# A block of x turned two steps behind its convolution, and column copies and the last row scaling placed ahead of the attention's steps

## The chip, the cores and the metric

One core of a Trainium2 chip runs the kernel. The metric is device microseconds of the whole program, the median of three runs: 4026.04 us (4020.71 to 4030.5). The engines are TensorE (PE, which multiplies and transposes into PSUM), VectorE (DVE), ScalarE (ACT), GpSimd (POOL) and SyncE (SP, which here only issues loads of weights). All data is 32-bit float.

## The reference, cut to what matters

The model is one large mixer layer with mixture-of-experts, followed by two smaller layers. The change lies in the mixer of the large layer. From the normed input h (512 tokens, 1024 wide, with 256 context tokens beside it) a projection makes, among others, x, B, C and z of a state-space branch (SSD) and q, k, v of a neighbourhood attention (NA).

```
xbc = silu(dwconv(xbc, conv_w, conv_b))       # 5-tap convolution along the tokens
xs, Bm, Cm = split(xbc)                       # xs: 2048 channels = 4 groups of 512
states, y   = chunked scan of xs, dt, A, Bm, Cm   # chunks of 128 tokens, both directions
u = y * silu(z);  u = u * rsqrt(mean(u*u) + eps)  # per group of 512: the row scaling
o_na = neighbourhood_attention(rope(q), rope(k), v, ...)   # 16 heads, 8 x 64 grid
```

The convolution runs along tokens, so x is made with channels on the partitions. The scan wants tokens on the partitions, so each block of 128 channels is transposed ("turned") afterwards.

## The kernel before, in words

Each engine has a program written out by hand, a chain of Python generators. `pace` advances a main generator (the scan's steps, later the attention's steps) and puts so many steps of a filler generator ahead of each main step, by a list (PLAN0, PLAN1). Every engine runs its own share of the same steps in the same order; semaphores tie them together. An engine executes its instructions in the order of its program, so whatever stands behind a waiting instruction waits too.

**SSD projections.** `pe_proj`, `act_proj` and `dve_proj` treat one group of 512 channels in eight steps: four steps of x (one per block of 128 channels) and four of z. A block i of x goes through: `pe_conv` on PE (16 products with the weights, 2 PSUM banks), `act_pad` on ACT (two copies to SBUF, L742 and L745), `dve_conv` on DVE (five instructions, L768 and L772), `act_silu` on ACT (L753, L756), `pe_turn_x` on PE (six transposes, 2 banks, L319), and then `dve_turn_x` (L987) and `act_turn_x` (L953), which copy the turned block out and free its two banks. After the blocks PE turns B (two banks, copied out by DVE at L1002), and multiplies z in four tiles (L307, one bank each).

**The scan** of the group before is the main work meanwhile: `pe_chunks`, `act_chunks`, `dve_chunks`, `pool_chunks`, fifteen steps per group. Five state steps are followed by ten steps n = 0 to 9. PLAN0 puts one filler step ahead of each of the first three state steps and ahead of n = 0, 2, 4, 6 and 8. The four x steps of the next group stand at n = 0, 2, 4, 6; its first z step stands at n = 8, and z tiles 1 to 3 at the state steps of its own scan. In step n DVE runs `dve_second(n-2)`, `dve_first(n)` and `dve_join(n-2)`. `dve_join` (L1303) waits for three additions of POOL (L1334, L1337, L1340), which wait for POOL's product M (L1324), which waits for ACT's exponential (L1149), which waits for a select of DVE (L1275) that stands behind the convolution of the same step. ACT squares the joined row (L1180) and then comes to the next silu. PE's `pe_second` (L1090) needs M, and its L1097 products feed `dve_second`. The first state product (L1061) needs x weighed by DVE (L1050), which needs all four turned blocks.

**PSUM.** There are eight banks. `open_bank` takes the least recently used one of a pool's banks and waits until its last user has been copied out. For group 0 the x steps use all eight banks; after the fifth step the list is set to the four banks 0 to 3 (PG1), while the scan uses 4 to 7. So from then on a tile takes the bank of the tile four places before it. The last tiles of a group in the order before are: x3 (2 banks), turned block 2 (2), B (2), z0, z1, turned block 3 (2), z2, z3. Group 0's `dt` work (`pe_dt`, `act_dt`, `dve_dt`) stands between its fifth and sixth step.

**Into the attention.** After the last scan step every engine runs what is left of the filler (the rope of q and k, number 1, rows 2 and 3), then the NA attention's steps. The V products (`pe_na_v`, at L307) need HTn, a copy of the input with its columns in another order: ACT makes the odd tiles (`act_by_blocks`, L1776) and DVE the even ones (`dve_by_blocks`, L1782), as the first thing of their V filler, in attention step 1. `dve_scale_z` (L1208 to L1218) scales the rows of the last SSD group in step 3, and PE then turns them (`pe_finish_last`, L319), with ACT copying each out (L1189). POOL fills the near tables (`pool_near_zero`, `pool_near_edge` L1738, `pool_near_mid` L1748) and then takes its last two rope products (L1583).

Of the kernel before, what the change touches and what calls it, by code (L numbers as in the profile page):

```python
# [189 lines left out]
def build(nc, A, out):  # L190
    ctx = ExitStack()
    with ctx:
# [738 lines left out]

        def pe_proj(pe, g, pool):
            for i in range(4):
                pe_conv(pe, ("x", g), i, pool)
                if i:
                    pe_turn_x(pe, g, i - 1, pool)
                yield
            pe.wait_ge(*at("conv", "BF", g))
            for part, n in ((0, 4), (4, 2)):
                pe_turn(pe, ("tb", g, part), pool, [BF[:, g, (part + c) * 128:(part + c + 1) * 128] for c in range(n)], "pe_turn")  # L940
            for n, _ in enumerate(pe_gemm(pe, ("z", g), 8, 512, range(4), lambda i, kt, w: HT[:, kt, i * 128:(i + 1) * 128],
                                          lambda i, kt, w: w, pool, "pe_z")):
                if n == 1:
                    pe_turn_x(pe, g, 3, pool)
                yield

# [9 lines left out]
        def act_proj(act, g):  # L956

            def silu(i):
                prev = ("tx", g, i - 2, 4) if i > 1 else ("tx", g - 1, i + 2, 4)
                before = [("full", prev)] if g or i > 1 else []  # L960
                if g == 0 and i == 1:
                    before = [("full", ("BF", 3, 2))]
                act_silu(act, ("x", g), i, 4 * g + i, xsF[i % 2][:, 0:512], xsF[i % 2][:, 512:768], before)

            for i in range(4):
                if i:
                    silu(i - 1)
                act_pad(act, ("x", g), i)
                if i:
                    act_turn_x(act, g, i - 1)  # L970
                yield
            silu(3)
            zs = zs2[g % 2]
            for i in range(4):
                act.wait_ge(*at("full", (("z", g), i)))
                if i == 0 and g > 1:
                    act.wait_ge(*at("full", ("fin", g - 2, 3)))
                act.activation(zs[:, i, :], PS.of((("z", g), i)), ACT.Silu, bias=0.0, scale=1.0).then_inc(
                    *up(S("act_z"), ("free", (("z", g), i)), ("zs", g, i)))
                if i == 1:  # L980
                    act_turn_x(act, g, 3)
                yield

# [5 lines left out]

        def dve_proj(dve, g):  # L990
            for i in range(4):
                if i == 1 and g > 1:
                    dve.wait_ge(*at("gone", g - 2, "pool"))
                    dve.wait_ge(*at("gone", g - 2, "pe"))
                if i:
                    dve_turn_x(dve, g, i - 1)
                dve_conv(dve, ("x", g), i, 4 * g + i)
                yield
            for part, n in ((0, 4), (4, 2)):
                key = ("tb", g, part)  # L1000
                dve.wait_ge(*at("full", key))
                dve.tensor_copy(BT2[g % 2][:, part:part + n, :], r3(PS.of(key)[:, 0:n * 128], 128)).then_inc(  # L1002
                    *up(S("dve_xs"), ("free", key), ("bt", g, part)))
            for i in range(4):
                if i == 1:
                    dve_turn_x(dve, g, 3)
                yield
# [342 lines left out]
        def act_finish_last(act):  # L1350
# [1 line left out]
            for part in range(2):  # L1352
                act_finish(act, 3, part)
            yield

        def dve_finish_last(dve):
            dve_scale_z(dve, 3)
            yield from idle(2)

# [460 lines left out]

        def act_na_v(act, m):
            if m == 0:
                act_by_blocks(act)
                act.wait_ge(*at("gone", 3, "pool"))
            for i in range(6):
                if i % 2:
                    key = (("v", m), i)
                    act.wait_ge(*at("full", key))  # L1830
                    act.activation(nv2[m][:, i, :], PS.of(key), ACT.Copy, bias=0.0, scale=1.0).then_inc(*up(S("act_v"), ("free", key), ("V", m, i)))
                yield
# [21 lines left out]
        def dve_na_v(dve, m):  # L1854
            if m == 0:
                dve_na_rope(dve, 1, 3)
                dve_by_blocks(dve)
                dve.wait_ge(*at("gone", 3, "pool"))
            for i in range(6):
                if i % 2 == 0:  # L1860
                    key = (("v", m), i)
                    dve.wait_ge(*at("full", key))
                    dve.tensor_copy(nv2[m][:, i, :], PS.of(key)).then_inc(*up(S("dve_v"), ("free", key), ("V", m, i)))
                yield
# [1182 lines left out]
        def act_program(act):  # L3047
            act_start(act)
            act_ssd_rows(act)
            weave(act_bc(act), act_ada_rest(act), 1)  # L3050
            proj = act_proj(act, 0)
            weave(take(proj, 5), act_dt(act), 0.5)
            filler = chain(proj, *[act_proj(act, g) for g in (1, 2, 3)], act_na_qk(act, 0), act_na_qk(act, 1))
            pace(chain(*[act_chunks(act, g) for g in range(4)]), filler, PLAN0, False)
            wait_all(act, CHUNKS_END)
            act.wait_ge(*at("rpb"))
            act.dma_start(ncon, nsrc).then_inc(*up(S("near_in"), by=16))
            act_near_raw(act, 0)
            V0 = act_na_v(act, 0)
            pace(act_att_2(act, NEAR), chain(filler, take(V0, 2), act_finish_last(act), V0, act_na_v(act, 1), act_na_qk(act, 2), act_na_qk(act, 3), act_branch_ssd(act)), PLAN1)  # L3060
            run(act_gates(act, "n", 1))
            act_out1(act)
            act_router(act)
            act_gather(act, 0)
            act_tables(act)
            for m in range(8):
                act_experts(act, m)
            act_moe_end(act)
            for L in range(2):
                if L == 0:  # L3070
                    act_first_of_0(act)
                else:
                    act_between(act)
                pace(act_att_2(act, CAUSAL[L]), chain(*[act_proj_2(act, L, n) for n in (1, 2, 3)]), PLAN2)
                act_last_out_2(act, L)
                if L:
                    act.wait_ge(*at("attn_end", L))
                    act.dma_start(gf, A["g_final"].partition_broadcast(128)).then_inc(*up(S("gf_in"), ("gf",), by=16))
                act_mlp(act, L)
            act_end(act)  # L3080

        def dve_program(dve):
            last_conv[0] = None
            dve_start(dve)
            dve_ssd_pads(dve)
            weave(dve_bc(dve), dve_ada_rest(dve), 1)
            proj = dve_proj(dve, 0)
            weave(take(proj, 5), dve_dt(dve), 0.5)
            filler = chain(proj, *[dve_proj(dve, g) for g in (1, 2, 3)], dve_na_qk(dve, 0), dve_na_qk(dve, 1, 0))
            pace(chain(*[dve_chunks(dve, g) for g in range(4)]), filler, PLAN0, False)  # L3090
            wait_all(dve, CHUNKS_END)
            V0 = dve_na_v(dve, 0)
            pace(dve_att_2(dve, NEAR), chain(filler, take(V0, 2), dve_finish_last(dve), V0, dve_na_v(dve, 1), dve_na_qk(dve, 2), dve_na_qk(dve, 3, 2), dve_branch_ssd(dve)), PLAN1)
            dve_branch_na(dve)
            dve_out1(dve)
            dve_router(dve)
            dve_places(dve, 0)
            dve_gather(dve, 0)
            for m in range(8):
                dve_experts(dve, m)  # L3100
            dve_moe_end(dve)
            for L in range(2):
                if L == 0:
                    dve_first_of_0(dve)
                else:
                    dve_between(dve)
                pace(dve_att_2(dve, CAUSAL[L]), chain(*[dve_proj_2(dve, L, n) for n in (1, 2, 3)], dve_out_2(dve, L)), PLAN2)
                dve_last_out_2(dve, L)
                dve_mlp(dve, L)
            dve_end(dve)  # L3110

        def pool_program(pool):
            pool_start(pool)
            filler = chain(idle(27), pool_na_qk(pool, 0), pool_na_qk(pool, 1))
            pace(chain(*[pool_chunks(pool, g) for g in range(4)]), filler, PLAN0, False)
            pool_near_zero(pool)
            pool_near_edge(pool, 0)
            pool_near_mid(pool, 0)
            pace(pool_att_2(pool, NEAR), chain(filler, idle(14), pool_na_qk(pool, 2), pool_na_qk(pool, 3), idle(20)), PLAN1)
            pool_branch_na(pool)  # L3120
            pool_out1(pool)
            pool_places(pool, 0)
# [51 lines left out]
```

## Time and profile before

| | |
|---|---|
| median of 3 runs | 4026.04 us |
| profiled execution | 4025.7 us, its span 4023.9 us |
| PE busy | 3660.3 us (91%) |
| DVE / ACT / POOL busy | 1148.0 / 772.9 / 441.4 us |
| mean granted clock of PE | 0.969 |

Times in the rows are microseconds from the span's start. A timeline row holds start, duration, engine, line, operation, tiles and count, and in brackets the idle time of that engine before it and what ended it. A product of one 128x128 block by 512 columns is recorded as two matmuls, so a tile of eight products shows x16. The granted clock is 1.00 at 2.4 GHz and 0.50 at 1.2 GHz. The change touches the stretch from about 215 to 810 us.

### The profile page before, as it was taken

The numbers are of one execution on the slowest core, as the hardware profiler recorded it, in microseconds if no ns is written. First come the engines' busy times: TensorE is split into PE (matmuls) and PEld (weight loads), VectorE is DVE, ScalarE is ACT, GpSimd is POOL, SyncE is SP. The second block draws the span as 40 slices with busy tenths as digits, with TensorE's granted clock in tenths as the row PEclk, the third lists the DMA queues.
The fourth block names the chain that finished last, engine by engine and source line by source line (L and its number), as shares of the span: only waits on it lengthen the run. The fifth ranks groups of instructions, "written<-read, shape, count | busy, mean of one in ns | idle before, by whom it ended". The sixth has DMA issues, their size and how long they took to land.

```text
span 4023.9 us, 32988 instructions
## 1 busy us (share of the span) xinstructions
PE 3660.3 (91%) x12600; PEld 1766.6 (44%) x12600; DVE 1148.0 (29%) x2602; ACT 772.9 (19%) x1778; POOL 441.4 (11%) x397
## 2 busy tenths in 40 slices
PE   6888899899999887888888888899999999999999
PEld 3355454444444433333233334555444445554444
DVE  2345555424210220311101114543221134432211
ACT  2024444322210200000000002332110123221100
POOL 1002223302100000000000001101221011012210
PEclk8899999999999999999999998999999999999999
DMA  8322223211222479999999991102222120022220
GB/s 253 126 72 79 69 84 94 69 58 37 79 71 96 174 283 409 409 409 409 409 409 409 409 392 54 37 27 84 84 77 75 57 84 32 32 96 67 84 71 34
DMA packets 302154, 634.08 MB, mean 158 GB/s; under 512 B 32499, under 2 KB 145763, under 8 KB 301743
## 3 DMA queue, kind: packets, MB, share of 16 engines
q1 hardware_dynamic: 240480, 591.96, 39.3%
q10 hardware_dynamic: 61519, 40.02, 3.6%
q8 instruction: 102, 1.67, 0.2%
q14 instruction: 53, 0.43, 0.0%
HBM read 625.50 MB, written 10.24 MB: 158 GB/s over the span
## 4 chain that ended last, share of the span: by engine, by line
PE 52%; DMA 19%; DVE 3%; ACT 1%; issue 1%; POOL 0%; SPq 0%; DVEq 0%; ACTq 0%
PE psum L307 26%; DMA arena<-in_w_exp_up_dram 7%; DMA arena<-in_w_exp_gate_dram 7%; PE psum L1572 6%; DMA arena<-in_w_exp_down_dram 4%; PE psum L2851 4%; PE psum L2815 4%; PE psum L2357 3%; PE psum L1396 2%; PE psum L2836 1%; PE psum L1424 1%; PE psum L2306 1%; PE psum L1405 1%; PE psum L2275 1%; PE psum L2750 1%
## 5 line engine op out<-in xcount | busy, mean ns | idle before, releaser
L307 PE MATMUL psum<-arena 128*128 128x512 f32 (+1 forms) x3200 | 1302.6, 565 | 7.6 <-DVE arena L1782 5.0
L307 PEld LDWEIGHTS psum<-arena 128*128 128x128 f32 x3200 | 609.8, 192 | 682.2 <-issue 653.6
L2357 PE MATMUL psum<-arena 128*64 128x512 f32 x3072 | 693.7, 596 | 153.0 <-DMA arena<-in_w_exp_up_dram 76.5
L2357 PEld LDWEIGHTS psum<-arena 128*64 128x64 f32 x3072 | 233.3, 136 | 594.6 <-issue 574.1
L1572 PE MATMUL psum<-arena 128*128 128x512 f32 x768 | 351.9, 613 | 0.0
L732 PE MATMUL psum<-arena 128*128 128x512 f32 (+1 forms) x768 | 269.8, 511 | 1.3 <-ACT arena L550 1.3
L1572 PEld LDWEIGHTS psum<-arena 128*128 128x128 f32 x768 | 147.5, 196 | 193.8 <-issue 192.9
L1504 DVE CUSTOM_DVE_ANT_0 arena<-psum,arena 128x512 f32<-128x512 f32 (+3 forms) x224 | 113.9, 546 | 387.0 <-PE psum L1396 386.8
L2894 POOL TENSOR_SCALAR arena<-arena 128x512 f32<-128x512 f32 x88 | 138.4, 1572 | 696.5 <-ACT arena L2873 696.5
L732 PEld LDWEIGHTS psum<-arena 128*128 128x128 f32 x768 | 151.0, 199 | 125.1 <-issue 114.5
L2900 DVE SCALAR_TENSOR_TENSOR arena<-arena 128x512 f32<-128x512 f32 x88 | 66.2, 753 | 426.5 <-POOL arena L2894 426.5
L1444 ACT ACTIVATE arena<-arena 128x512 f32<-128x512 f32 (+3 forms) x224 | 134.3, 601 | 138.5 <-DVE arena L1504 137.9
L2422 DVE TENSOR_TENSOR arena<-arena,psum 128x512 f32<-128x512 f32 x32 | 22.0, 689 | 461.7 <-PE psum L2357 461.7
L2851 PE MATMUL psum<-arena 128*128 128x512 f32 x352 | 152.0, 592 | 0.0
L2815 PE MATMUL psum<-arena 128*128 128x512 f32 x352 | 151.7, 592 | 0.0
L2873 ACT ACTIVATE arena<-psum 128x512 f32<-128x512 f32 x88 | 52.5, 597 | 509.8 <-PE psum L307 478.3
L1405 PE MATMUL psum<-arena 128*128 128x128 f32 x576 | 86.1, 278 | 56.0 <-DVE arena L1511 30.7
L1583 POOL TENSOR_TENSOR arena<-arena 128x512 f32<-128x512 f32 x48 | 62.3, 1300 | 588.0 <-ACT arena L1579 588.0
L319 PE MATMUL psum<-arena 128*128 128x128 f32 (+2 forms) x442 | 68.0, 303 | 61.6 <-ACT arena L756 27.4
L1405 PEld LDWEIGHTS psum<-arena 128*128 128x128 f32 x576 | 68.8, 143 | 107.1 <-DVE arena L1511 38.1
L2815 PEld LDWEIGHTS psum<-arena 128*128 128x128 f32 x352 | 66.6, 189 | 84.7 <-issue 84.7
L1396 PE MATMUL psum<-arena 64*128 64x512 f32 (+6 forms) x448 | 103.4, 543 | 0.0
(283 smaller groups left out, 2946.7 us busy)
## 6 DMA issues: line engine op xcount, KB each, us to landing
arena<-in_w_exp_gate_dram SPq DMA_DIRECT2D x128, 1024.0 KB, 18.8
arena<-in_w_exp_up_dram SPq DMA_DIRECT2D x128, 1024.0 KB, 18.5
arena<-in_w_exp_down_dram SPq DMA_DIRECT2D x128, 1024.0 KB, 18.8
arena<-in_w_in_dram SPq DMA_DIRECT2D x64, 1024.0 KB, 5.3
arena<-in_w_up_dram SPq DMA_DIRECT2D x88, 512.0 KB, 4.8
arena<-in_w_ada_dram SPq DMA_DIRECT2D x24, 1024.0 KB, 8.5
arena<-in_w_down_dram SPq DMA_DIRECT2D x20, 1024.0 KB, 5.1
arena<-acs_scratch ACTq DMA_DIRECT2D x64, 256.0 KB, 3.7
```

What stands on the lines that cost most here:

```text
L307: mm = pe.matmul(shaped(b, l, r), l, r, start=kt == 0, stop=kt == nkt - 1)
L319: t = pe.transpose(b[0:m, c * k:(c + 1) * k], x, ident[0:k, 0:k])
L732: mm = pe.matmul(b[:, 0:z - a], wt(nm, kt, 512)[:, i * 128:(i + 1) * 128], HT[:, kt, a:z], start=kt == 0, stop=kt == 7)
L1396: pe.matmul(b[:, 0:u.nk], J.queries(u, a, z), J.keys(u, a, z), start=True, stop=True).then_inc(*up(S("pe_score"), ("full", ("s2", J.id, i, ...
L1405: t = pe.transpose(b[:, 128 * j:128 * j + 128], J.score(i, c)[:, 128 * j:128 * j + 128], ident)
L1444: act.activation(J.score(i, c), J.score(i, c), ACT.Exp, bias=sv2(i, c)[:, 0:1], scale=-1.0, accum_out=sv2(i, c)[:, 1:2]).then_inc(*up(S("a ...
L1504: dve.tensor_tensor_reduce(out=J.score(i, c), in0=PS.of(("s2", J.id, i, c))[:, 0:u.nk], in1=J.table(u, c), scale=-J.scale(u), scalar=3.0e3 ...
L1572: mm = pe.matmul(b, wt(nm, kt, 256)[:, i * 128:(i + 1) * 128], src[:, kt, 0:512], start=kt == 0, stop=kt == 7)
L2357: mm = pe.matmul(banks[n][64 * j:64 * j + 64, :], lhs[:, kt, 64 * j:64 * j + 64], w, start=kt == 0, stop=kt == 2 * nkb - 1)
L2815: mm = pe.matmul(banks[i], actT[:, kt, i * 128:(i + 1) * 128], wt(nm, kt, 512), start=kt == 0, stop=kt == 21)
L2851: mm = pe.matmul(b, actT[:, kt, i * 128:(i + 1) * 128], wt(nm, kt, 512), start=kt == 0, stop=kt == 21)
L2894: pool.tensor_scalar(accs3[n % 4], pads3[n % 4][:, 0:512], w3(L, 0, ti_of(s, i)), None, ALU.mult).then_inc(*up(S("pool_acc"), ("acc3", L, n)))
```

## The change

In `pe_proj`, `act_proj` and `dve_proj` block i-2 is turned at step i, before block i's own convolution (on PE) or pad copies (on ACT) or convolution (on DVE), instead of block i-1 after or before it. Block 2 is turned at the start of the fifth step. PE and ACT turn block 3 with z tile 0, in the fifth step; DVE copies its share of block 3 in the sixth step, as before. The column copies move from the V filler to ahead of the attention, behind the near tables' loads on ACT; on DVE the row scaling of the last group moves there too, behind the copies. POOL takes one rope product ahead of the near tables and one behind them, before the attention's first step.

```diff
         def pe_proj(pe, g, pool):
             for i in range(4):
+                if i > 1:
+                    pe_turn_x(pe, g, i - 2, pool)
                 pe_conv(pe, ("x", g), i, pool)
-                if i:
-                    pe_turn_x(pe, g, i - 1, pool)
                 yield
+            pe_turn_x(pe, g, 2, pool)
             pe.wait_ge(*at("conv", "BF", g))
...
-                if n == 1:
+                if n == 0:
                     pe_turn_x(pe, g, 3, pool)
...
             for i in range(4):
                 if i:
                     silu(i - 1)
+                if i > 1:
+                    act_turn_x(act, g, i - 2)
                 act_pad(act, ("x", g), i)
-                if i:
-                    act_turn_x(act, g, i - 1)
                 yield
             silu(3)
+            act_turn_x(act, g, 2)
...
-                if i == 1:
+                if i == 0:
                     act_turn_x(act, g, 3)
...
         def dve_proj(dve, g):
             for i in range(4):
-                if i == 1 and g > 1:
+                if i == 2 and g > 1:
                     dve.wait_ge(*at("gone", g - 2, "pool"))
                     dve.wait_ge(*at("gone", g - 2, "pe"))
-                if i:
-                    dve_turn_x(dve, g, i - 1)
+                if i > 1:
+                    dve_turn_x(dve, g, i - 2)
                 dve_conv(dve, ("x", g), i, 4 * g + i)
                 yield
+            dve_turn_x(dve, g, 2)
...
-        def dve_finish_last(dve):
-            dve_scale_z(dve, 3)
-            yield from idle(2)
...
         def act_na_v(act, m):
             if m == 0:
-                act_by_blocks(act)
...
         def dve_na_v(dve, m):
             if m == 0:
                 dve_na_rope(dve, 1, 3)
-                dve_by_blocks(dve)
...
             act_near_raw(act, 0)
+            act_by_blocks(act)
...
+            dve_by_blocks(dve)
+            dve_scale_z(dve, 3)
             V0 = dve_na_v(dve, 0)
-            pace(dve_att_2(dve, NEAR), chain(filler, take(V0, 2), dve_finish_last(dve), V0, ...
+            pace(dve_att_2(dve, NEAR), chain(filler, take(V0, 2), idle(2), V0, ...
...
             pool_near_zero(pool)
+            run(take(filler, 1))
             pool_near_edge(pool, 0)
             pool_near_mid(pool, 0)
-            pace(pool_att_2(pool, NEAR), chain(filler, idle(14), ...), PLAN1)
+            run(take(filler, 1))
+            pace(pool_att_2(pool, NEAR), chain(filler, idle(14), ...), [0] + PLAN1[1:])
```

## Rows read from the trace of the kernel before

**Rows 1.** The page's first part: busy time, share and instructions.
```profile
PE 3660.3 (91%) x12600; PEld 1766.6 (44%) x12600; DVE 1148.0 (29%) x2602; ACT 772.9 (19%) x1778; POOL 441.4 (11%) x397
```

**Rows 2.** The waits of PE, 240 to 840 us: total, times, longest.
```profile
PE psum L319 <- ACT arena L756: 27.4, 9, 4.9
...
PE psum L1061 <- DVE arena L1050: 5.5, 4, 1.4
PE psum L319 <- DVE arena L1218: 5.3, 1, 5.3
PE psum L307 <- DVE arena L1782: 5.0, 1, 5.0
```

**Rows 3.** Timeline, 340 to 350 us: from silu 0 of group 1 to the next convolution.
```profile
345.99 0.49 ACT L756 ACTIVATE arena<-arena 128x256 f32<-128x256 f32 x1
...
346.87 0.37 ACT L745 ACTIVATE arena<-psum 128x256 f32<-128x256 f32 x1
...
347.69 0.69 DVE L987 COPY arena<-psum 128x512 f32<-128x512 f32 x1 [9.35 <-PE psum L319]
...
348.30 0.61 DVE L768 TENSOR_SCALAR arena<-arena 128x772 f32<-128x772 f32 x1
```

**Rows 4.** Timeline of DVE: what follows the join at n = 7, groups 1, 2, 3.
```profile
403.32 1.01 DVE L1002 COPY arena<-psum 128x512 f32<-128x512 f32 x2
...
525.17 1.01 DVE L1002 COPY arena<-psum 128x512 f32<-128x512 f32 x2
...
646.59 1.01 DVE L1002 COPY arena<-psum 128x512 f32<-128x512 f32 x2
```

**Rows 5.** Timeline of PE: B turned, z0, second 6 and 7 with L1097, z1 of group 2.
```profile
517.37 0.82 PE L319 MATMUL psum<-arena 128*128 128x128 f32 x6
518.03 7.04 PE L307 MATMUL psum<-arena 128*128 128x512 f32 x16
524.91 1.89 PE L1090 MATMUL psum<-arena 128*128 128x64 f32 x16
...
528.41 7.04 PE L307 MATMUL psum<-arena 128*128 128x512 f32 x16
```

**Rows 6.** Timeline of PE: z0 of group 1, and the first state products of groups 1, 2, 3.
```profile
392.90 7.05 PE L307 MATMUL psum<-arena 128*128 128x512 f32 x16
...
416.40 1.99 PE L1061 MATMUL psum<-arena 128*128 128x512 f32 x4 [1.39 <-DVE arena L1050]
...
537.49 1.99 PE L1061 MATMUL psum<-arena 128*128 128x512 f32 x4 [1.38 <-DVE arena L1050]
...
659.73 1.99 PE L1061 MATMUL psum<-arena 128*128 128x512 f32 x4 [1.39 <-DVE arena L1050]
```

**Rows 7.** Timeline of PE and DVE, 288 to 298 us: z1 and first state of group 0, end of `dve_dt`.
```profile
288.61 7.04 PE L307 MATMUL psum<-arena 128*128 128x512 f32 x16
...
297.69 1.99 PE L1061 MATMUL psum<-arena 128*128 128x512 f32 x4 [1.38 <-DVE arena L1050]
...
292.02 0.43 DVE L916 TENSOR_TENSOR arena<-arena 128x256 f32<-128x256 f32 x1 [0.58 <-ACT arena L868]
```

**Rows 8.** Timeline, 765 to 804 us: into the attention.
```profile
765.17 2.35 POOL L1738 TENSOR_SCALAR arena<-arena 128x128 f32<-128x128 f32 x4 [4.93 <-DMA arena<-rpb_copies]
...
776.40 2.23 ACT L1776 ACTIVATE arena<-arena 128x512 f32<-128x512 f32 x4
...
779.25 9.09 PE L307 MATMUL psum<-arena 128*128 128x512 f32 x16 [5.04 <-DVE arena L1782]
...
799.90 0.71 ACT L1444 ACTIVATE arena<-arena 128x512 f32<-128x512 f32 x1
...
801.93 1.67 DVE L1218 TENSOR_SCALAR arena<-arena 128x512 f32<-128x512 f32 x4
...
803.66 3.62 PE L319 MATMUL psum<-arena 128*128 128x128 f32 x16 [5.25 <-DVE arena L1218]
```

**Rows 9.** Busy time of PE in a window: length, busy (count), granted clock, DMA share, GB/s.
```profile
779.00:784.00 5.00, 4.75 (x7) 0.58 0.00 0
```

More of the change, by code:

```diff
@@ L3091, in dve_program @@
             wait_all(dve, CHUNKS_END)
+            dve_by_blocks(dve)
+            dve_scale_z(dve, 3)
             V0 = dve_na_v(dve, 0)
-            pace(dve_att_2(dve, NEAR), chain(filler, take(V0, 2), dve_finish_last(dve), V0, dve_na_v(dve, 1), dve_na_qk(dve, 2), dve_na_qk(dve, 3, 2), dve_branch_ssd(dve)), PLAN1)
+            pace(dve_att_2(dve, NEAR), chain(filler, take(V0, 2), idle(2), V0, dve_na_v(dve, 1), dve_na_qk(dve, 2), dve_na_qk(dve, 3, 2), dve_branch_ssd(dve)), PLAN1)
             dve_branch_na(dve)
@@ L3116, in pool_program @@
             pool_near_zero(pool)
+            run(take(filler, 1))
             pool_near_edge(pool, 0)
             pool_near_mid(pool, 0)
-            pace(pool_att_2(pool, NEAR), chain(filler, idle(14), pool_na_qk(pool, 2), pool_na_qk(pool, 3), idle(20)), PLAN1)
+            run(take(filler, 1))
+            pace(pool_att_2(pool, NEAR), chain(filler, idle(14), pool_na_qk(pool, 2), pool_na_qk(pool, 3), idle(20)), [0] + PLAN1[1:])
             pool_branch_na(pool)
```

## The prediction, written before the result was known

> **What bounds the kernel now.** I read the page's first part, then the waits of PE in the stretch that the change touches, then the timelines of PE, DVE, ACT and POOL around each wait. PE is busy 91% of the span [rows 1], so what a change here is worth is what it does to PE's waits and to its clock. Between 240 and 840 us nine waits of PE for ACT's silu (L756) cost 27.4 us, four for DVE's weighing 5.5 us, one for the row scaling 5.3 us, and one for the column copies 5.0 us [rows 2]. The question is what is late next at each.
>
> **The silu waits are the visible end of a loop, not a late instruction.** While PE waits for silu i, the loop that made it late runs silu, pad, convolution (DVE), select, exponential (ACT), M and three additions (POOL), join (DVE), square (ACT), next silu. PE stands in it at one link only. Silu 0 of group 1 ends at 346.48 and the pad copies of block 1 at 347.24; DVE's convolution could start then, but DVE first waits for PE's turn of block 0 and copies it (347.69), so it starts at 348.30 [rows 3]. With the turn two steps behind, DVE finds its turned block long done and waits for the pad alone. That takes 348.30 - 347.24 = 1.06, less some 0.05 of start, so 1.0 us out of the loop at block 1. At blocks 2 and 3 ACT's copy of a turned block now stands ahead of the pad; it is as large as the second pad copy, 0.37 [rows 3], so 0.65 is left at block 2. At block 3 I take 0.3, between 0 and 0.65, since the turn there can run at full clock and was cheaper. Together the loop ends 1.95 us earlier per group (bounds 1.0 to 3.2, three times the first). The 27.4 us are therefore not recovered: PE runs ahead, and waits at the next place where it needs the loop.
>
> **Where that place is.** It is the bank of z0. The tile four places before z0 is the first half of turned block 2, in either order of the program; z0 waits for DVE's copy of it. Before, that copy stood in DVE's fourth step, ahead of convolution 3, and z0 of group 1 started at 392.90 [rows 6]. After, it is the first instruction of DVE's fifth step, at n = 8, and DVE comes to it only behind the join of n = 7, which ends at 403.3, 525.2 and 646.6 in the three groups (the B copies start right behind it) [rows 4]. So z0 starts at the join's end less 1.95, plus one copy of about 0.65 (L987 takes 0.69 [rows 3]). For group 1 that is 402.0 instead of 392.90. Queued behind it on PE are turn 3, second 6 and 7, and z1. These take, start to start: z0 524.91 - 518.03 = 6.88, turn 0.66, second 6 and 7 with their L1097 products 528.41 - 524.91 = 3.50, z1 6.88, together 17.9 us at full clock [rows 5].
>
> PE has then been idle for more than ten microseconds. What that does to the clock is bounded by the V tile behind a wait of 5.04: it took 9.09 instead of 7.04 [rows 8, 5], the granted clock being 0.58 over its first 5 us [rows 9], that is mostly the lower level of 1.2 GHz. I take those 2.05 us for z0; the lower bound is 0, the upper a whole tile at 1.2 GHz, 6.9.
>
> The first state product follows z1 at once: its DVE wait of 1.4 [rows 6] goes, since block 3 is turned a tile earlier and DVE's copy, join and weighing of group end run beside z1. So state 0 comes 0.65 + 17.9 + 2.05 = 20.6 us behind the join's new end. Before, it came 416.40 - 403.32 = 13.1, 537.49 - 525.17 = 12.3 and 659.73 - 646.59 = 13.1 behind it [rows 4, 6]. The differences, less 1.95 each, are +5.6, +6.35 and +5.55 us: 17.5 us slower for groups 1 to 3. If DVE's copy did not gate z0, this would be the other sign; that is a rival below.
>
> The Trainium skill (PSUM — Partial Sum Buffer, § Engine vs sequencer instructions) says that the queues of ScalarE, VectorE and GpSimdE are strict first-in first-out. By that rule the 0.69 us copy cannot pass the join that waits for POOL; the rows show the copies at L1002 behind the join in all three groups, so the trace agrees. The same skill (Perfetto Trace Analysis, § Identifying Performance Opportunities) says that the same gap repeating on the engine that should be saturated can mean too few buffers. For the nine waits of today the trace says otherwise, their releaser is the silu and not a copy that frees a bank; by the rule, a fifth bank would be worth their 27.4 us now, by the row nothing.
>
> **Group 0** has eight banks for its first five steps. The order after is ..., z0, turned block 3 (banks 0, 1), ac, atot, acT, and then z1 from banks 0 to 3: the oldest is bank 0, turned block 3's. Its DVE copy stands in the sixth step, behind all of `dve_dt`, which ends at 292.45 [rows 7]. Convolution 3 and `dve_dt` come some 0.6 earlier, as a copy of 0.69 leaves the place ahead of them. So z1 starts at 291.85 + 0.65 = 292.5 instead of 288.61, ends 6.88 + 2.05 later at 301.4 (the same clock price, PE having idled some 4.6 us), and state 0 follows at once: 301.4 against 297.69 [rows 7] is +3.7 us (bounds +1.0 with neither clock price nor a late `dve_dt`, and +8.5 at 1.2 GHz throughout). SP's program and the loads of weights are not touched; the slots are freed by the same products, later by as much as PE is.
>
> **The column copies.** DVE and ACT are free of the scan before the last two rope steps, while PE still has two tiles of q and k. ACT's four copies (2.23 [rows 8]) stand ahead of the rope's raw copy, which comes as much later; DVE's rope waits for it, and so does POOL's. POOL takes that product ahead of the edge additions, which started at 765.17 [rows 8], so the near tables come some 1.5 to 2 us later and still ahead of the first scores (whose products ended where the V tile's wait began, 779.25 - 5.04 = 774.2). Should the tables be late, DVE's first scores are late, not PE's V tile, which has 7 us of work. So the V tile starts behind the scores: the wait of 5.04 goes and the clock price of 2.05 with it, -7.1 us (bounds -5.0 to -7.3).
>
> **The row scaling.** The last wait of 5.25 goes too, and the 16 turns run at full clock: PE spent 5.25 + 3.45 = 8.7 us there, from 798.4. But the fourth tile of turns needs the bank of the first (three banks), which ACT frees; ACT is busy with exponentials to 799.90 + 0.71 = 800.6 [rows 8], 2.2 us behind the scores, and then needs 0.7 for its copy (as that exponential of the same size) and PE 0.45 for the last turn, with up to 1 for two loads that ACT issues between. That is 3.9 us instead of 8.7: -4.8 (bounds -3.5 and -7.0). DVE's 1.67 us of scaling with five tiny operations and the 4 copies lie in DVE's idle time ahead of the first scores; without that cover they would delay the rope by some 4 us and PE not at all.
>
> **The sum.** +3.7 + 17.5 - 7.1 - 4.8 = +9.3 us on the profiled execution's own time of 4025.7, which is the median to within 0.4: 4035. All of it is ahead of the experts' stage, whose loads wait for the end of the mixer, so it passes through one to one.
>
> **The rivals.** (1) *The bank does not hold z0 that long; PE's waits simply go.* This is the other side: 27.4 + 5.5 saved in the projections and 11.9 in the attention, 4025.7 - 44.8 = 3981. For it: the nine waits are real. Against: the loop without PE's link is only 1 us shorter. It decides if the join of n = 7 ended before PE turns B, ten microseconds earlier than in the rows. (2) *The same hold, smaller*: the loop loses 3.2 us per group instead of 1.95, and PE stays at 2.4 GHz behind the holds. That gives 9.3 - 3.7 - 4 x 2.05 = -2.6, 4023: no change. (3) *The clock*: PE runs the whole tile behind each hold at 1.2 GHz, 4 x (6.9 - 2.05) = +19.4, 4054. (4) *The attention's start gives nothing back*, because the near tables or ACT's turns become late: +21.2, 4047.
>
> **How the numbers follow.** Forecast 0.50, its own range 4028 to 4044; (1) 0.10, (2) 0.22, (3) 0.06, (4) 0.12. The measurement tells from no change what is over 0.2%, 8 us: above 4034 or below 4018. The forecast lies near that line: I give 0.34 of its 0.50 to slower and 0.16 to the same. (2) is the same with 0.14, faster with 0.08. So slower 0.34 + 0.06 + 0.12 = 0.52, same 0.30, faster 0.18. The range of 4016 to 4050 leaves out (1) and most of (3).
>
> **What would show it.** Right: L307 with a wait of 12 to 15 us for DVE L987 three times (z0) and once of 4 to 5 us (z1 of group 0); no waits of L319 for L756 of over 2 us; new waits of L1090 for POOL's L1324 of 1 to 4 us ahead of the second of each pair; z0 at 9 us; the V tile at 7.0 with no wait. Wrong: z0 within 2 us of the turned B, or state 0 of group 1 before 416; or a new wait for L1525 or L1189 of over 3 us in the attention.

## The result, and the profile after

The changed kernel takes 4044.23 us (median of 8 runs, 4039.15 to 4047.54) against 4031.19 us for the one before (8 runs): a ratio of 1.0034, 95% interval 1.0021 to 1.0047, so 13.7 us slower, 8.5 to 18.9. The prediction was 9.3 us slower, and slower had its largest chance (0.52). As a time the forecast was 4035, with a range of its own of 4028 to 4044; 4044.23 lies 0.2 us outside that range and inside the wider one of 4016 to 4050. The kernel before, 4026.04 us in three runs, had a median of 4031.19 in the eight runs of this comparison, so the difference is the fairer measure. In a second comparison, beside `z0_bank` and `act_order` below, the ratio of the changed kernel was 1.0031 (1.0019 to 1.0043).

The waits of PE, 240 to 860 us of the changed kernel (total, times, longest), answer to [rows 2]. Line numbers behind 935 have moved by one to three: DVE's copy of the turned block, L987, is L989 now, the state product L1061 is L1064, `pe_second` L1090 is L1093, the select L1275 is L1278, DVE's last instruction ahead of the join, L1294, is L1297, the join L1303 is L1306, M L1324 is L1327 and POOL's last addition L1340 is L1343.

```profile
PE psum L307 <- DVE arena L989: 44.3, 4, 13.8
PE psum L1093 <- POOL arena L1327: 21.6, 9, 3.6
PE psum L319 <- ACT arena L756: 4.2, 3, 2.5
PE psum L1064 <- DVE arena L1244: 3.2, 7, 0.7
PE psum L319 <- DVE arena L1244: 1.8, 3, 0.6
PE psum L319 <- ACT arena L1192: 1.8, 1, 1.8
PE psum L844 <- DVE arena L897: 1.7, 1, 1.7
```

The silu waits fell from 27.4 to 4.2 us, and those for the weighing, the row scaling and the column copies are gone. In their place four z tiles (L307) wait 44.3 us for DVE's copy of a turned block, and PE's second products wait nine times for M, 21.6 us in all, where before they waited twice, 3.2 us:

```profile
PE psum L1090 <- POOL arena L1324: 3.2, 2, 2.1
```

The timeline of PE around z0 of group 1 in the changed kernel (start, duration, what, and in brackets the idle time before):

```profile
327.36 10.48 PE L732 MATMUL psum<-arena 128*128 128x512 f32 x32
...
388.84 1.44 PE L1093 MATMUL psum<-arena 128*128 128x64 f32 x8 [3.58 <-POOL arena L1327]
390.07 3.33 PE L1100 MATMUL psum<-arena 128*128 128x512 f32 x4
393.24 1.47 PE L319 MATMUL psum<-arena 128*128 128x128 f32 x12
408.52 9.52 PE L307 MATMUL psum<-arena 128*128 128x512 f32 x16 [13.82 <-DVE arena L989]
417.88 0.82 PE L319 MATMUL psum<-arena 128*128 128x128 f32 x6
418.54 1.90 PE L1093 MATMUL psum<-arena 128*128 128x64 f32 x16
420.27 1.94 PE L1100 MATMUL psum<-arena 128*128 128x512 f32 x4
422.04 7.04 PE L307 MATMUL psum<-arena 128*128 128x512 f32 x16
428.92 1.88 PE L1064 MATMUL psum<-arena 128*128 128x512 f32 x4
```

And DVE in the same place. Block 2 and the B blocks are turned by 394.7, but DVE reaches the copy of block 2 only behind the join (L1306), which waits for POOL:

```profile
393.59 0.62 DVE L768 TENSOR_SCALAR arena<-arena 128x772 f32<-128x772 f32 x1 [3.65 <-ACT arena L745]
394.25 4.20 DVE L772 SCALAR_TENSOR_TENSOR arena<-arena 128x772 f32<-128x772 f32 x4
...
401.44 0.98 DVE L1278 COPY_PREDICATED arena<-arena 128x512 f32<-128x512 int32 x1
406.13 1.74 DVE L1306 TENSOR_TENSOR arena<-arena 128x512 f32<-128x512 f32 x1 [3.72 <-POOL arena L1343]
407.79 0.68 DVE L989 COPY arena<-psum 128x512 f32<-128x512 f32 x1
408.39 1.01 DVE L1005 COPY arena<-psum 128x512 f32<-128x512 f32 x2
```

z0 starts at 408.52, as the copy ends. PE was free from 394.7 on. Group 0's hold is at its z1. At the attention's start the two waits of [rows 8] are gone, and one for ACT's copy of a turned tile has come:

```profile
289.48 1.06 PE L319 MATMUL psum<-arena 128*64 128x128 f32 x4
294.51 10.21 PE L307 MATMUL psum<-arena 128*128 128x512 f32 x16 [3.97 <-DVE arena L989]
304.55 1.88 PE L1064 MATMUL psum<-arena 128*128 128x512 f32 x4
...
799.67 1.13 PE L1395 MATMUL psum<-arena 64*128 64x512 f32 x4
800.73 7.15 PE L307 MATMUL psum<-arena 128*128 128x512 f32 x16
...
817.88 1.53 PE L319 MATMUL psum<-arena 128*128 128x128 f32 x12
821.18 0.66 PE L319 MATMUL psum<-arena 128*128 128x128 f32 x4 [1.77 <-ACT arena L1192]
```

Where the 14.5 us between the two profiled spans (4023.9 and 4038.4) lie, from the timelines of PE of both:

| stretch | before | after | difference | predicted |
|---|---|---|---|---|
| start to group 0's first convolution (untouched) | 215.86 | 218.05 | +2.2 | 0 |
| from there to state 0 of group 0 | 81.83 | 86.50 | +4.7 | +3.7 |
| group 1: first convolution to state 0 | 95.79 | 101.56 | +5.8 | +5.6 |
| group 2 | 94.51 | 100.71 | +6.2 | +6.35 |
| group 3 | 95.66 | 102.01 | +6.35 | +5.55 |
| state 0 of group 3 to the first scores | 113.35 | 115.09 | +1.7 | 0 |
| first scores to the fourth | 35.01 | 22.97 | -12.0 | -11.9 |
| the rest (between groups, and behind 823) | | | -0.4 | 0 |

The first and the sixth row are what single executions differ by: over the eleven profiled executions of all kernels here the first convolution came at 214.2 to 219.2, and the sixth stretch took 112.5 us in a second execution of the changed kernel. The rows in between are steadier: in that second execution groups 1 to 3 took 101.56, 100.72 and 101.96 us.

### The profile page after: what moved, and what is told of

Same layout as the page of the kernel before. It is cut to its first block, busy times and chain, and to the rows that moved or that the text cites. A ratio compares the mean times of both kernels' runs of the same rounds, so it can differ in the third digit from the quotient of the medians.

```text
span 4038.4 us, 32988 instructions
## 1 busy us (share of the span) xinstructions
PE 3655.3 (91%) x12600; PEld 1754.9 (43%) x12600; DVE 1147.1 (28%) x2602; ACT 771.0 (19%) x1778; POOL 442.5 (11%) x397
## 4 chain that ended last, share of the span: by engine, by line
PE 52%; DMA 18%; DVE 3%; SPq 1%; ACT 1%; issue 1%; POOL 0%; DVEq 0%; ACTq 0%
PE psum L307 26%; DMA arena<-in_w_exp_up_dram 7%; DMA arena<-in_w_exp_gate_dram 7%; PE psum L1571 6%; DMA arena<-in_w_exp_down_dram 4%; PE psum L2848 4%; PE psum L2812 4%; PE psum L2354 3%; PE psum L1395 2%; PE psum L1423 1%; PE psum L2833 1%; PE psum L2303 1%; PE psum L1404 1%; SPq L276 1%; PE psum L2747 1%
## 5 line engine op out<-in xcount | busy, mean ns | idle before, releaser
L307 PE MATMUL psum<-arena 128*128 128x512 f32 (+1 forms) x3200 | 1309.4, 568 | 46.9 <-DVE arena L989 44.3
L307 PEld LDWEIGHTS psum<-arena 128*128 128x128 f32 x3200 | 612.3, 193 | 726.7 <-issue 658.9
L1571 PEld LDWEIGHTS psum<-arena 128*128 128x128 f32 x768 | 145.8, 193 | 189.9 <-issue 189.0
L732 PEld LDWEIGHTS psum<-arena 128*128 128x128 f32 x768 | 150.5, 199 | 121.8 <-issue 110.8
L1404 PEld LDWEIGHTS psum<-arena 128*128 128x128 f32 x576 | 68.8, 143 | 107.1 <-DVE arena L1510 38.1
L2812 PEld LDWEIGHTS psum<-arena 128*128 128x128 f32 x352 | 66.6, 189 | 84.7 <-issue 84.7
L2848 PEld LDWEIGHTS psum<-arena 128*128 128x128 f32 x352 | 66.5, 189 | 83.8 <-issue 83.8
```

The costliest lines, as they stand in the source:

```text
L307: mm = pe.matmul(shaped(b, l, r), l, r, start=kt == 0, stop=kt == nkt - 1)
L732: mm = pe.matmul(b[:, 0:z - a], wt(nm, kt, 512)[:, i * 128:(i + 1) * 128], HT[:, kt, a:z], start=kt == 0, stop=kt == 7)
L1404: t = pe.transpose(b[:, 128 * j:128 * j + 128], J.score(i, c)[:, 128 * j:128 * j + 128], ident)
L1571: mm = pe.matmul(b, wt(nm, kt, 256)[:, i * 128:(i + 1) * 128], src[:, kt, 0:512], start=kt == 0, stop=kt == 7)
L2812: mm = pe.matmul(banks[i], actT[:, kt, i * 128:(i + 1) * 128], wt(nm, kt, 512), start=kt == 0, stop=kt == 21)
L2848: mm = pe.matmul(b, actT[:, kt, i * 128:(i + 1) * 128], wt(nm, kt, 512), start=kt == 0, stop=kt == 21)
```

## The experiments

All were timed in five rounds beside the kernel before. Microseconds gained or lost against the kernel before are worked out from the ratio. "Group sum" is the time from first convolution to state 0, groups 1 to 3 together, in the one profiled execution: 285.96 before, 304.28 in the changed kernel. Two executions with the same projections differ in it by up to 1 us (285.96 before and 286.94 in `attn_only`).

**The two parts apart.** `attn_only` has the projections of the kernel before and the rest of the change; `proj_only` the reverse.

```diff
 # attn_only, against the changed kernel (act_proj and dve_proj likewise)
         def pe_proj(pe, g, pool):
             for i in range(4):
-                if i > 1:
-                    pe_turn_x(pe, g, i - 2, pool)
                 pe_conv(pe, ("x", g), i, pool)
+                if i:
+                    pe_turn_x(pe, g, i - 1, pool)
                 yield
...
```

> Only the column copies, the row scaling and POOL's rope products are moved; the SSD projections are those of the kernel before. Theory (the two parts are independent, the loss is all in the projections): the waits of L307 for L1782 (5.0) and of L319 for L1218 (5.3) go and only one of 1.8 us for ACT's L1192 copy remains; 12 us faster than before, about 0.3%. Rival (the gain of 12 us seen at the attention's start in the changed kernel is only there because the later scan left the other engines ahead of PE): under 5 us faster, with new waits of PE in the attention.

> Only the SSD projections are changed; the start of the attention is that of the kernel before. Theory: four waits of L307 for DVE's copy of a turned block, 44 us together, and PE's waits for the silu nearly gone; 22.6 us slower than before (4.7 for group 0, 5.7 + 6.1 + 6.2 for groups 1 to 3), at most 24.4 if the 1.7 us of group 3's scan belong to it, about 0.6%. Rival (the loss is smaller and the rest is between the parts): under 16 us.

Measured: `attn_only` 0.9968 (0.9956 to 0.9979), 12.9 us faster than before at 4028.27; `proj_only` 1.0063 (1.0050 to 1.0075), 25.4 us slower, one above the 24.4 that were the most expected, with an interval of 20 to 30. Both rivals are out, and the two parts add up: +25.4 - 12.9 = +12.5. In `attn_only` the one new wait of PE in the attention is 1.8 us for ACT's copy L1189; in `proj_only` L307 waits four times for L989, 44.4 us.

**The place of one copy.** `copy2`, the changed kernel with one edit, moves DVE's copy of turned block 2 from the head of the fifth step to behind convolution 3.

```diff
                 dve_conv(dve, ("x", g), i, 4 * g + i)
+                if i == 3:
+                    dve_turn_x(dve, g, 2)
                 yield
-            dve_turn_x(dve, g, 2)
```

> The changed kernel with DVE's copy of turned block 2 behind its convolution 3 (in the fourth step) instead of at the head of the fifth. Theory (z0 is held by that copy behind the join): z0 of group 1 starts some 9.5 us earlier against its first convolution, the wait of L307 for the copy falls from 12.7 to 13.8 us to 3 to 5 us; what comes next late is turn 3, which waits for silu 3 some 4 us; state 0 comes 4 to 5 us earlier per group, 12 to 15 us in all, 0.3% faster than the changed kernel and as fast as the one before within 0.1%. Group 0's hold of 4 us stays. Rival (z0 waits for the loop as a whole, not for the place of one copy; the copy's 0.6 us then only lengthens the loop): the wait of z0 stays over 12 us, and the kernel is 1 to 2 us slower than the changed one.

Measured: 1.0014 (1.0005 to 1.0023), 4033.11 us, 5.6 us slower than before, where as fast as before within 0.1% was expected. The timeline of PE in `copy2`, group 1, whose first convolution started at 326.86:

```profile
393.62 2.36 PE L319 MATMUL psum<-arena 128*128 128x128 f32 x12
398.70 8.84 PE L307 MATMUL psum<-arena 128*128 128x512 f32 x16 [2.73 <-DVE arena L989]
411.69 0.85 PE L319 MATMUL psum<-arena 128*128 128x128 f32 x6 [4.15 <-ACT arena L954]
412.37 3.40 PE L1094 MATMUL psum<-arena 128*128 128x64 f32 x16
415.57 3.73 PE L1101 MATMUL psum<-arena 128*128 128x512 f32 x4
```

z0 starts 71.8 us behind the first convolution, against 81.2 in the changed kernel: 9.3 earlier, the theory's 9.5. Turn 3 then waits 4.15 us, as expected, for a bank that ACT frees behind silu 3. But the group sum fell by 5.0 (299.27), not by 12 to 15. The products behind that second wait took 3.40 and 3.73 instead of 1.90 and 1.94. The granted clock over the two was 0.52 and 0.50. So 3.3 us went to the lower clock, in work that the single long hold had left at full clock; in groups 2 and 3 it was 3.4 and 3.1. Together these 9.8 us are what the gain fell short by (7 to 10). As a ratio the gain over the changed kernel is some 0.17 to 0.20%, 7 to 8 us.

**Block 3 turned as before.** `copy2_turn3` is `copy2` with block 3 turned with z tile 1 again; `turn3_only` has that edit alone.

```diff
-                if n == 0:
+                if n == 1:
                     pe_turn_x(pe, g, 3, pool)
...
-                if i == 0:
+                if i == 1:
                     act_turn_x(act, g, 3)
```

> As copy2, and block 3 turned with z tile 1 on PE and ACT, as in the kernel before. Theory: no wait for silu 3; z0 starts as in copy2, M 7 is late by 0 to 1 us, z1, turn 3 and the wait of 1.4 us for the weighing as before: state 0 some 8 us earlier per group than in the changed kernel (2 to 3 us earlier than in the kernel before), and z1 of group 0 takes turned block 2's bank again, so the hold of 4 us there goes; 28 to 30 us faster than the changed kernel, 15 to 17 us (0.4%) faster than the one before. Rival (the loop decides, wherever block 3 is turned): within 5 us of copy2.

> The changed kernel with block 3 turned with z tile 1, as before; the copy of block 2 stays behind the join. Theory: z1 of group 0 takes turned block 2's bank, its hold of 4 us and its clock price go (4.7 us), while z0 of groups 1 to 3 is held 12.7 to 13.8 us as in the changed kernel and each group gets back the weighing's wait of 1.4 us and a turn of 0.66 behind z1: 0 us against the changed kernel, plus or minus 2. Rival (the early turn of block 3 is what holds z0): 30 us faster than the changed kernel, like copy2_turn3.

Measured: `copy2_turn3` 0.9953 (0.9941 to 0.9966), 4009.79 us, 19 us faster than before (14 to 24; 15 to 17 were expected); group sum 281.91, and group 0 back at 81.81. Per group that is 7.5 less than in the changed kernel, for which 8 was expected. `turn3_only` 1.0018 (1.0008 to 1.0027): its z0 is held as before (38.9 us in three waits), group 0 gets back 5.1 us and the groups lose 3.4 (307.70). The profile agrees with the 0 plus or minus 2 us of the theory (-1.7). The ratio lies 0.13 to 0.16%, 5 to 6 us, below the changed kernel's, with intervals that overlap; whether these microseconds are real stays open. The rival, 30 us, is out in either.

**The bank alone.** `z0_bank`, the changed kernel with one edit, changes no instruction's place on any engine. z0 of groups 1 to 3 takes the least recently used of all eight banks, and turn 3 behind it takes the bank that z0 had.

```diff
-                b = open_bank(pe, (nm, i), pool)
+                b = open_bank(pe, (nm, i), PALL if nm[0] == "z" and nm[1] and i == 0 else pool)
```

> The changed kernel, with one edit in the choice of banks: z0 of groups 1 to 3 takes the least recently used of all eight banks (one of the scan's, freed by DVE in step n = 7 ahead of the join) instead of one of banks 0 to 3. No instruction of any engine changes its place. Theory (z0 waits for the bank of turned block 2, not for its inputs): z0 starts some 6 to 7 us earlier, its wait for DVE L989 is replaced by one of 6 to 8 us for DVE L1297; turn 3 then takes the bank that z0 had and waits for the same copy and for silu 3, some 2 us. State 0 comes 1 to 4 us earlier per group, 3 to 12 us in all. Rival (z0 is late for another reason, its weights or PE's own order): z0 starts where it did, within 1 us.

Measured: 0.9974 (0.9965 to 0.9983), 4017.75 us: some 23 us faster than the changed kernel, 4041.45 in the same comparison. The timeline of PE in `z0_bank`, group 1, first convolution at 324.57:

```profile
390.45 1.48 PE L319 MATMUL psum<-arena 128*128 128x128 f32 x12
398.78 9.58 PE L307 MATMUL psum<-arena 128*128 128x512 f32 x16 [6.86 <-DVE arena L1297]
408.32 0.88 PE L319 MATMUL psum<-arena 128*128 128x128 f32 x6
409.04 1.90 PE L1093 MATMUL psum<-arena 128*128 128x64 f32 x16
```

The releaser is the one expected, with the wait halved; z0 starts 74.2 us behind the first convolution instead of 81.2, and the group sum is 284.70, 19.5 less. The expectation was 3 to 12, a miss: by the time the tile ends, silu 3 and both copies that turn 3 needs are done, so there is no second wait and no second fall of the clock, and nearly all of the 7 us per group arrives at state 0 (6.5). The choice of this one bank makes the changed kernel 10 us faster than the kernel before (0.26%) instead of 13.7 slower. So in the changed kernel z0 waited for its bank: it can start at least 7 us earlier with the inputs that it has.

**Is it the loop?** `one_behind` keeps the turn one step behind, as before, and only moves DVE's copy behind its convolution; its attention part is the changed one. The edit as against `attn_only`:

```diff
-                if i:
-                    dve_turn_x(dve, g, i - 1)
                 dve_conv(dve, ("x", g), i, 4 * g + i)
+                if i:
+                    dve_turn_x(dve, g, i - 1)
```

> The projections' order of the kernel before (block i-1 turned at step i) with one change: DVE copies turned block i-1 behind its convolution i instead of ahead of it; the attention part as changed (12 us faster than before by itself). Theory (the silu waits are the end of a loop, from which taking PE's turn and DVE's copy out saves 1.0 us per block, whatever the lag of the turn on PE): each loop is 1.0 us shorter less the 0.6 of the copy where it comes ahead of the select, so 0.4 to 1.0 us per block, 9 blocks: 4 to 9 us faster than attn_only, 16 to 21 us (0.4 to 0.5%) faster than before, about as fast as copy2_turn3. Rival (only the turn two steps behind takes PE off the loop): within 2 us of attn_only.

Measured: 0.9978 (0.9969 to 0.9986), 9 us faster than before where 16 to 21 were expected, and against 0.9968 of `attn_only` in another comparison no gain: the rival's side. The timeline of DVE in `one_behind`:

```profile
349.00 0.62 DVE L768 TENSOR_SCALAR arena<-arena 128x772 f32<-128x772 f32 x1 [8.92 <-ACT arena L745]
349.66 4.20 DVE L772 SCALAR_TENSOR_TENSOR arena<-arena 128x772 f32<-128x772 f32 x4
353.78 0.68 DVE L987 COPY arena<-psum 128x512 f32<-128x512 f32 x1
...
355.05 0.74 DVE L1275 COPY_PREDICATED arena<-arena 128x512 f32<-128x512 int32 x1
```

The convolution does start 1.0 us earlier behind silu 0 (0.8 instead of 1.8 [rows 3]), but the copy now stands ahead of the select and takes 0.6 of it back. The group sum is 285.72 against 286.94 in `attn_only` and 285.96 before: 1.2 us at most, hardly more than two executions differ by, where I had expected 4 to 9. The join of n = 7 came 0.5 to 1.0 us earlier behind the first convolution than in `attn_only`, against 2.2 to 2.4 us in the changed kernel. So moving DVE's wait alone shortens the loop by less than half of what the turn two steps behind does, and PE's silu waits stayed (31.8 us, 30.9 in `attn_only`).

**ACT's copies off the loop.** `act_order` is `copy2_turn3` with ACT's copies behind its pad copies and ahead of silu 3.

```diff
-                if i > 1:
-                    act_turn_x(act, g, i - 2)
                 act_pad(act, ("x", g), i)
+                if i > 1:
+                    act_turn_x(act, g, i - 2)
                 yield
-            silu(3)
             act_turn_x(act, g, 2)
+            silu(3)
```

> copy2_turn3 with two more moves on ACT: its copies of turned blocks 0 and 1 stand behind the pad copies of blocks 2 and 3 instead of ahead of them, and its copy of turned block 2 ahead of silu 3. Theory: the loop loses another 0.36 us at blocks 2 and 3, and z1's wait of 1.1 us for that copy goes: 0.7 + 1.0 us per group, 3 to 5 us faster than copy2_turn3. Rival (PE's clock takes it back, or the pad copies were not what the loop waits for): within 1 us of copy2_turn3.

Measured: 0.9961 (0.9948 to 0.9973), `copy2_turn3` 0.9953 in an earlier comparison: not told apart. In the profiled execution the group sum is 279.47 against 281.91, 2.4 us less where 3 to 5 were expected. z1's wait is gone, and the join of n = 7 starts 0.6 us earlier behind the first convolution in each of the three groups, so the loop is shorter. Part of it went to the clock, as the rival has it: the three z0 tiles took 28.3 us together against 24.5. The profile leans to the theory and the timing can't confirm it; open. The changed kernel in the comparison of `z0_bank` and `act_order`:

> The changed kernel itself, on the chip of the two others, to have its ratio beside theirs: 1.0034 again, between 1.0021 and 1.0047.

It gave 1.0031 (1.0019 to 1.0043).

## Why the prediction was right

**What bounds.** The reading of the nine silu waits as the end of a loop held. The joins start so many us behind the first convolution of their group, before and after:

| join in step | group 1 | group 2 | group 3 | earlier, mean | forecast |
|---|---|---|---|---|---|
| n = 3 | 41.49, 40.45 | 41.35, 40.48 | 41.65, 40.56 | 1.0 | 1.0 |
| n = 5 | 62.21, 60.24 | 61.65, 60.27 | 61.72, 60.37 | 1.6 | 1.65 |
| n = 7 | 81.06, 78.77 | 80.53, 78.80 | 80.85, 78.90 | 2.0 | 1.95 |

The loop lost 2.3, 1.7 and 1.95 us, forecast 1.95. PE ran ahead and waited for M nine times, 21.6 us in all: seven times 2.5 to 3.6 us, as the text named it, and twice under 0.2. One sign named in the prediction failed: a wait of turn 3 for silu 3 of over 2 us came once (2.47, group 0).

**The hold of z0.** Forecast 12 to 15 us three times and 4 to 5 once; measured 13.82, 12.72, 13.80 and 3.97. `copy2` and `z0_bank` show it from two sides: one moves the copy, the other the bank, and z0 starts 9.3 and 7 us earlier. Both are needed for the hold: the copy that stands behind the join, and the bank that waits for this copy.

**The clock price** was the term that was sized too small. I took 2.05 us at each hold. The tiles took 10.21 (group 0), 9.52, 8.65 and 9.85 instead of 7.04: 3.2, 2.5, 1.6 and 2.8, together 10.1 instead of 8.2. That accounts for the projections' part of the miss: group 0 and groups 1 to 3 came 23.0 us later, forecast 21.2. In group 0 it is the whole of the 1.0 us. The granted clock of PE behind two of the holds (window, length, busy, clock, DMA share, GB/s):

```profile
294.00:299.00 5.00, 4.49 (x6) 0.50 0.12 26
299.00:304.00 5.00, 5.00 (x11) 0.83 0.00 0
...
408.00:413.00 5.00, 4.48 (x6) 0.50 0.00 0
413.00:418.00 5.00, 5.00 (x14) 0.96 0.00 0
```

It is the lower level of 1.2 GHz at first, and 2.4 GHz again before the tile ends, so rival (3), a whole tile at 1.2 GHz, fell.

**Group 0.** The hold by `dve_dt` came as worked out (3.97 us). Turn 3 behind z0 waited 2.47 us for silu 3; that cost nothing, since PE's next wait, for `dt` work of DVE (L897), fell from 5.7 to 1.7 us.

**The column copies and the row scaling.** Forecast -7.1 and -4.8, measured -12.0 together. The wait for ACT's copy at the fourth tile of turns was forecast at some 2 us, and is 1.77. Rival (4), nothing given back, fell with `attn_only`.

**The rivals.** (1), PE's waits simply go, did not happen, yet the projections could be made faster than before: with the copy off the hold and block 3 turned late, `copy2_turn3` is 19 us ahead of the kernel before, 12 to 13 of them from the attention. Even there the groups gain 4.1 us together, not the 32.9 of rival (1): PE still waits 23.8 us for M and 11.0 us for the bank of z0. The 2 us left of the 19 have no place in the profile. (2), a smaller hold, would have needed the loop to lose 3.2 us and the clock to stay up; it lost 2.0, and the clock fell.

**What is not explained.** The 14.5 us between the spans hold 2.2 from ahead of any changed instruction and 1.7 from the sixth stretch, which a second execution does not show. Without both 10.6 remain, 1.3 above the forecast. The ratio puts the loss at 13.7 us, and where the other 3 lie no profile shows; its interval reaches down to 8.5. So the mechanism is confirmed stretch by stretch, while that the total lay this near to 9.3, and clear of no change, had some luck in it: the forecast itself stood only 1.3 us above the 8 us that it took for the limit.

## What to carry to other kernels

A wait that repeats once per block is often the visible end of a loop over several engines. Moving the waiting instruction back lets its engine run ahead, and the gain is only what leaves the loop (here 2.0 us per group, where the waits were 9.1); the rest turns into new waits. Before moving a consumer of a buffer, ask which later tile takes the buffer that it frees, and what stands ahead of the freeing copy in its new place: here a copy of 0.68 us behind a join held PE 13 us, and a different bank for one tile won back 19.5 us with no instruction moved. Two short idle stretches can cost more clock than one long one: in group 1 5.1 us in `copy2` against 2.5 in the changed kernel.

## What the runs showed of the hardware

The price in clock did not grow with the idle time. Behind 3.97 us of idle a tile of 16 took 3.2 us longer, behind 12.72 us 1.6 us, behind 13.8 us 2.5 and 2.8. Nor is it fixed for one length: in `act_order` three waits of 4.1 us cost 2.9, 2.5 and 1.8 us, and in `copy2_turn3` one of 3.58 us cost 0.1. In `copy2` 2.73 and 4.15 us of idle, with a tile between them, left the next twenty small products at the lower level (3.40 + 3.73 against 1.90 + 1.94 us). What decides between these prices no run here shows.

DVE's join of 512 columns takes 1.73 to 1.75 us where it starts together with POOL's M product, and 0.69 where POOL is idle. In both kernels that splits the 16 joins of the four scans without exception, 10 against 6, and of the slow ones nine, three in each of the first three scans, lie on the loop. In the changed kernel POOL's instruction beside that join is this one:

```profile
406.06 1.27 POOL L1327 TENSOR_TENSOR arena<-arena 128x512 f32<-128x512 f32 x1
```
